# Output stage of a hybrid attention step: loads in another order, x rows filled into y earlier, seven piece places

## The chip, the cores and the metric

The kernel runs on one core of a Trainium2 chip. The metric is the device time of one execution, in microseconds (us). The kernel before took 1928.67 us as the median of three runs (1927.08 to 1930.82). The profile comes from one further execution, which took 1934.61 us; the span of its trace is 1932.9 us.

The engines are called by the names of the profile: PE is TensorE (matmul), DVE is VectorE, ACT is ScalarE, POOL is GpSimd, and SP is SyncE, which here does nothing but wait and issue DMAs. SPq and POOLq are the queues on which SP and POOL issue theirs.

## What is computed

One layer of a trunk, for 1024 new tokens (prompt) and 32 tokens of a running stream (sample), width 2048, all in float32:

```python
hp = rms_norm(y_prompt, norm_pre[l])
mp, st_p = mixers_prompt(hp, w_in[l], attn_sinks[l], rel_bias[l], slopes)
y_prompt = y_prompt + rms_norm(jnp.einsum('btm,md->btd', mp, w_out[l]), norm_post[l])
# the same for y_sample, with the caches of keys and values
```

The mixers project with `w_in` and run three groups of heads: A (stick-breaking attention over the whole past, 12 heads), B (a sliding window with 12 query and 4 key heads) and C (a band of chunks, 8 heads). Each head output is gated by a SiLU. The gated rows are the input of the product with `w_out`. The outputs are `y_prompt`, `y_sample` and twelve tensors of keys and values.

## The kernel before, in words

**Units and ticks.** The attention works two heads at a time: six units of A, then four of C, then six of B. PE runs the projection with `w_in` without a pause, and the attention steps of a unit are placed between its pieces. Python tables give each step a time in ticks, twelve to a projected tile, and the functions `pe_plan`, `act_plan`, `dve_plan` and `sp_plan` sort each engine's instructions by these times. A time only sets the order in the program. When an instruction runs is decided by the semaphores it waits for, and each engine takes its instructions strictly in order.

**The output stage.** After the last tile (`TICKS`) comes the product of the mixed rows (tokens by 2048) with `w_out`. It is cut into two by two blocks and made with seven block products in place of eight (`ORDER`, `LEFT`, `RIGHT`): five of the seven need a sum or difference of two blocks of `w_out`. Each block product is two stages of 512 output columns, each stage is eight *pieces* of 128 inner rows, so there are 14 x 8 = 112 pieces. I call them piece 0 to 111, and "time P(r)" is when PE starts piece r. Stages 0 and 1 are product 3, stages 2 and 3 product 6, then 1, 2, 4, 5 and 7. The last eight pieces (from `TAIL0` = 104) run by another order, with their own buffers (`tail_raw`).

For one piece PE does four groups of three matmuls (`out_mm(r, j)`, j = 0 to 3, one for each 128 tokens): float32 is split into a high and a low part, and hi x hi, hi x lo and lo x hi are added up in PSUM. A stage uses four of seven PSUM banks in turn. So the group j = 3 of a stage's first piece writes the bank which j = 0 of the stage just finished has left, and it must wait until ACT has copied that bank (`copied`, semaphore `c_copied`) or DVE has added it to the result (`added`, `c_added`).

**The path of a piece.** SP loads 256 KB of `w_out` into a place of a ring (`piece_out`: `w_raw` for places 0 to 3, `r_extra` for the rest, `R_RING` = 6 in all), and for products with a sum a second 256 KB into `b_out` (`B_RING` = 5). DVE adds the two (`summed_out`), ACT makes the high part (`high_out`), DVE the low part (`low_out`), and PE waits for it (`operands_out`). SP may load piece r when PE is done with piece r - `R_RING` (`wait_used`).

**What else is loaded.** The mixed rows come back from a scratch tensor in nine loads (`mixed_load`, tile `raw`; places 0 to 7 of it are the first half of the inner dimension, 8 to 15 the second). Products 3 and 6, the pieces 0 to 31, read places 0 to 7 only. The sample tokens are multiplied apart: after 16 of the pieces (`SAMPLE_AFTER`) PE runs `sample_out(v)` with 1 MB of `w_out` rows (`rows_out`, tile `w_s`, one buffer). `post_gains` loads the weights of the last norm. `fill_y` copies x rows 512 to 1023 and the sample rows from DRAM to DRAM into y, because for these rows POOL later adds the normed product onto y with an accumulating DMA (`add_y`). For rows 0 to 511 x is loaded (`residual`) and added by DVE (`finish`).

**What sets the order around the change.** `output_tasks` gives every step of the output stage its time. `piece_out_at(r)` and `mixed_at(n)` are the times of the loads on SP, `at_piece(r)` is the time of piece r. `FINISH` is the order in which token tiles are completed (`TT` is the sample).

## Time and profile before

| what | value |
|---|---|
| median of three runs | 1928.67 us |
| the profiled execution, and its span | 1934.61 us, 1932.9 us |
| PE busy in the span | 1891.8 us (98%) |
| DVE, ACT, POOL busy | 1246.4, 673.4, 56.7 us |
| DMA queues: SP's (q1), POOL's (q0) | 64.5%, 2.2% of 16 engines |
| first matmul of the output stage | at 1578.70 us |
| last busy time of PE | ends at 1924.17 us |

Most of the time PE is busy, at full clock. The views to read are therefore those of the few places where it is not: its idle gaps, the granted clock behind them, and what was late there. "DMA share" in a row by stretches is the mean busy share of the core's 16 DMA engines, and GB/s is what they moved.

### The profile page before, as it was taken

How to read it: one execution, taken by the hardware profiler on the slowest of the kernel's cores; microseconds unless marked ns; L12 is line 12 of the kernel's file. 1: busy time of each engine (PE TensorE's matmuls, PEld its weight loads, DVE VectorE, ACT ScalarE, POOL GpSimd, SP SyncE). 2: the span in 40 equal slices, each digit the busy share in tenths (PEclk: the TensorE clock that was granted, in tenths of full speed). 3: DMA queues.
4: the chain of work that ended last, by engine and by line, in shares of the span. 5: the costliest groups of instructions: out<-in, count | busy, mean ns of one | idle time of the engine just before them, and what ended most of it. 6: DMA issues, size and time to landing. Idle time of an engine off the chain costs nothing.

```text
span 1932.9 us, 31215 instructions
## 1 busy us (share of the span) xinstructions
PE 1891.8 (98%) x12592; PEld 1735.3 (90%) x12592; DVE 1246.4 (64%) x2235; ACT 673.4 (35%) x1235; POOL 56.7 (3%) x119
## 2 busy tenths in 40 slices
PE   6999999999999999999999999999999999999998
PEld 5999999999999999999999999999999987776776
DVE  7368787887878778454454444465445576765878
ACT  7233334343334334122222122233223353334463
POOL 4000000000000000000000000000000000000150
PEclk9999999999999999999999999999999999999999
DMA  6456777776776777666657666465446568766696
GB/s 245 117 121 137 161 159 163 147 152 150 150 163 149 164 149 162 140 140 153 134 126 158 138 141 136 113 147 126 101 100 135 135 246 313 242 228 240 222 256 229
DMA packets 887368, 318.35 MB, mean 165 GB/s; under 512 B 623417, under 2 KB 850505, under 8 KB 883881
## 3 DMA queue, kind: packets, MB, share of 16 engines
q1 hardware_dynamic: 884152, 307.64, 64.5%
q0 software_dynamic: 3072, 8.73, 2.2%
q8 instruction: 99, 1.62, 0.4%
q14 instruction: 45, 0.36, 0.1%
HBM read 227.23 MB, written 96.20 MB: 167 GB/s over the span
## 4 chain that ended last, share of the span: by engine, by line
PE 85%; DVE 9%; DMA 3%; ACT 2%; issue 1%; SPq 0%; POOL 0%; DVEq 0%
PE ps L1277 21%; PE ps L1278 20%; PE ps L1279 20%; PE ps L1471 4%; PE ps L1472 4%; PE ps L1473 4%; PE ps L1369 3%; PE ps L1449 3%; PE ps L1419 2%; PE ps L1341 2%; DVE arena L1956 1%; DMA r_extra<-in_w_out_dram 1%; DMA b_out<-in_w_out_dram 1%; DVE act_lo L1823 1%; DVE arena L1816 1%
## 5 line engine op out<-in xcount | busy, mean ns | idle before, releaser
L1277 PE MATMUL ps<-act_hi,w_hi 128*128 128x352 f32 x2688 | 877.8, 327 | 0.8 <-DVE arena L1856 0.8
L1279 PE MATMUL ps<-act_hi,w_lo 128*128 128x352 f32 x2688 | 863.1, 321 | 0.0
L1278 PE MATMUL ps<-act_lo,w_hi 128*128 128x352 f32 x2688 | 862.8, 321 | 0.0
L1277 PEld LDWEIGHTS ps<-act_hi,w_hi 128*128 128x128 f32 x2688 | 504.4, 188 | 21.0 <-issue 15.7
L1278 PEld LDWEIGHTS ps<-act_lo,w_hi 128*128 128x128 f32 x2688 | 505.4, 188 | 0.0
L1279 PEld LDWEIGHTS ps<-act_hi,w_lo 128*128 128x128 f32 x2688 | 504.4, 188 | 0.0
L1583 ACT ACTIVATE w_hi<-w_raw 128x512 fp32r<-128x512 f32 x224 | 139.4, 624 | 371.7 <-DMA w_raw<-in_w_in_dram 371.5
L1831 DVE TENSOR_TENSOR w_lo<-w_raw,w_hi 128x512 fp32r<-128x512 f32 x224 | 150.4, 672 | 52.8 <-ACT w_hi L1583 52.5
L1650 ACT ACTIVATE arena<-arena,small 128x257 f32<-128x257 f32 (+6 forms) x180 | 101.3, 565 | 198.2 <-DVE small L1994 198.2
L2154 DVE STREAM_TRANSPOSE arena<-arena 128x1024 f32<-128x1024 f32 (+4 forms) x100 | 132.5, 1325 | 38.3 <-ACT arena L1772 37.5
L1772 ACT ACTIVATE arena<-arena 128x1024 f32<-128x1024 f32 (+1 forms) x60 | 61.1, 1019 | 236.4 <-DVE arena L1968 236.4
L1471 PE MATMUL ps<-w_hi,l_hi 128*128 128x512 f32 x280 | 114.0, 407 | 10.4 <-DVE w_lo L2046 3.6
L1472 PE MATMUL ps<-w_lo,l_hi 128*128 128x512 f32 x280 | 111.9, 400 | 0.0
L1473 PE MATMUL ps<-w_hi,l_lo 128*128 128x512 f32 x280 | 111.5, 398 | 0.0
L1994 DVE CUSTOM_DVE_ANT_0 arena<-ps,arena 128x640 f32<-128x640 f32 (+5 forms) x72 | 44.0, 660 | 82.0 <-PE ps L1369 82.0
L1944 DVE TENSOR_TENSOR arena<-ps,arena 128x1024 f32<-128x1024 f32 (+1 forms) x60 | 70.3, 1172 | 29.7 <-ACT arena L1768 29.7
L1859 DVE COPY arena<-ps 128x352 f32<-128x352 f32 x84 | 43.1, 514 | 63.2 <-PE ps L1279 61.6
L1471 PEld LDWEIGHTS ps<-w_hi,l_hi 128*128 128x128 f32 x280 | 54.2, 193 | 31.5 <-issue 15.6
L1956 DVE TENSOR_TENSOR_SCAN arena<-arena 128x512 f32<-128x512 f32 (+4 forms) x102 | 79.5, 833 | 0.8
L1662 ACT ACTIVATE w_hi<-w_raw 128x512 fp32r<-128x512 f32 x70 | 44.0, 629 | 100.7 <-DVE w_raw L2031 84.1
L1764 ACT ACTIVATE arena<-ps 128x1024 f32<-128x1024 f32 (+1 forms) x60 | 58.4, 974 | 51.0 <-DVE ps L1938 40.5
L1768 ACT ACTIVATE arena<-arena 128x1024 f32<-128x1024 f32 (+1 forms) x60 | 61.1, 1019 | 40.7 <-DVE arena L2172 40.3
(173 smaller groups left out, 2073.2 us busy)
## 6 DMA issues: line engine op xcount, KB each, us to landing
w_raw<-in_w_in_dram SPq DMA_DIRECT2D x176, 256.0 KB, 3.4
weight_scratch<-arena SPq DMA_DIRECT2D x216, 128.0 KB, 3.4
arena<-weight_scratch SPq DMA_DIRECT2D x54, 512.0 KB, 4.6
b_out<-in_w_out_dram SPq DMA_DIRECT2D x72, 256.0 KB, 4.3
w_raw<-in_w_out_dram SPq DMA_DIRECT2D x70, 256.0 KB, 3.0
w_s<-in_w_out_dram SPq DMA_DIRECT2D x16, 1024.0 KB, 7.4
w_raw<-in_w_in_dram SPq DMA_DIRECT2D x96, 128.0 KB, 3.1
weight_scratch<-arena SPq DMA_DIRECT2D x80, 132.0 KB, 4.0
```

Source lines behind the costliest of these rows:

```text
L1277: mm(bank(g, GN), wh, ah, start=(k == 0), stop=False)
L1278: mm(bank(g, GN), wh, al, start=False, stop=False)
L1279: last = mm(bank(g, GN), wl, ah, start=False, stop=(k == KT - 1))
L1471: mm(out, th, wh, start=first, stop=False)
L1472: mm(out, th, wl, start=False, stop=False)
L1473: last = mm(out, tl, wh, start=False, stop=end)
L1583: fn(w_hi[:, q, :], w_raw[:, q, :], ACT.Copy).then_inc(hi_made, 1)
L1650: fn(s, s, ACT.Exp, bias=neg_max[0:rows_of(m), t:t + 1], scale=-1.0, accum_out=row_sum[0:rows_of(m), t:t + 1]).then_inc(p_exp, 1)
L1831: v.tensor_tensor(w_lo[:, slot, :], w_raw[:, slot, :], w_hi[:, slot, :].bitcast(F32), ALU.subtract).then_inc(lo_made, 1)
L1944: v.tensor_tensor(both, z, both, ALU.max).then_inc(sp_ready, 1)
L1956: v.tensor_tensor_scan(along, along, along, 0.0 if newest else carry[:, 2 * m - 8 + h:2 * m - 7 + h], ALU.add, ALU.max).then_inc(sum_ready, 1)
L2154: v.transpose(s, s).then_inc(wt_blocks, 1)
```

## The change

The diff does six things.

1. Five of the nine loads of mixed rows (places 8 to 15) move from the times of pieces 1 to 5.9 to those of pieces 8.2 to 17.2, and the load of the norm weights from 9.1 to 30.2.
2. The copies of x rows into y leave SP and the time of pieces 50 to 55. POOL issues them as eight copies of 512 KB and the small sample one while the C units run, each after a certain step of attention (`pv_done`).
3. The ring of pieces has seven places instead of six, so that from piece 10 on each load stands one piece earlier in SP's order, and so do its sum and its low part on DVE and its high part on ACT.
4. The group j = 3 of a stage's first piece is issued after the groups j = 0 to 2 of the second piece.
5. The sample visits come after pieces 15, 19, ..., 75 (every fourth) and not 10, 15, ..., 85 (every fifth); the sample is finished before tiles 4 to 7 and not after them, and takes the inner rows in plain order.
6. The first four loads of x for the last sum (`residual`) move from the times of pieces 99.5 to 102.5 to those of 86.2 to 90.7, 1.5 pieces apart.

```diff
@@ -282,7 +282,7 @@
         return (TICKS - 9, TICKS - 6, TICKS - 3, TICKS, TICKS + 0.2, TICKS + 0.4)[r]
     if r >= TAIL0:
         return at_piece(90.4 + 1.1 * (r - TAIL0))
-    return at_piece(max(r - 5, 2.6 + 0.3 * (r - 6)))
+    return at_piece(max(r + 1 - R_RING, 2.6 + 0.3 * (r - 6)))
 
 
 def summed_at(r):
@@ -290,7 +290,7 @@
 
 
 def mixed_at(n):
-    return (TICKS - 8.9, TICKS - 8.8, TICKS - 5.9, TICKS - 5.8, at_piece(1), at_piece(1.2), at_piece(1.4), at_piece(1.6), at_piece(5.9))[n]
+    return (TICKS - 8.9, TICKS - 8.8, TICKS - 5.9, TICKS - 5.8, at_piece(8.2), at_piece(10.2), at_piece(12.2), at_piece(14.2), at_piece(17.2))[n]
 
 
 def first_left_at(k):
@@ -363,7 +363,7 @@
                 plan.append((at + (1.7 if i else 0.8), "left_lo", i, k))
     for n in range(KT):
         if engine == "sp":
-            plan.append((sample_at(n - 1) if n else at_piece(6), "rows_out", 0, n))
+            plan.append((sample_at(n - 1) if n else at_piece(9.5), "rows_out", 0, n))
     for n in range(NCH):
         if engine == "act":
             plan.append((sample_at(KT - 1) + 0.1 * n, "sample_copy", 0, n))
@@ -396,9 +396,8 @@
                 plan.append((at + 1.2 + 0.1 * half, "add_y", t, half))
     if engine == "sp":
         plan += [(mixed_at(n), "load_mixed", 0, n) for n in range(len(MIXED_LOADS))]
-        plan += [(at_piece(104.3 + 0.1 * n if n > 3 else 99.5 + n), "residual", 0, n) for n in range(len(PLAIN))]
-        plan += [(at_piece(50 + 2.5 * n), "fill_y", 0, n) for n in range(3)]
-        plan += [(at_piece(3.9), "store_mixed", NU - 1, 0), (at_piece(9.1), "post_gains", 0, 0)]
+        plan += [(at_piece(104.3 + 0.1 * n if n > 3 else 86.2 + 1.5 * n), "residual", 0, n) for n in range(len(PLAIN))]
+        plan += [(at_piece(4.2), "store_mixed", NU - 1, 0), (at_piece(30.2), "post_gains", 0, 0)]
     return plan
 
 
@@ -511,9 +510,10 @@
 STAGES = 14
 PIECES = KH * STAGES
 TAIL0 = PIECES - KH
-R_RING, B_RING = 6, 5
+R_RING, B_RING = 7, 5
 LEAD = 3
-FINISH = (4, 5, 6, 7, TT, 0, 1, 2, 3)
+FILLS = 2 * NC
+FINISH = (TT, 4, 5, 6, 7, 0, 1, 2, 3)
 PLAIN = tuple((t, half) for t in range(4) for half in (0, 1))
 ADDED = [(t, half) for t in FINISH for half in (0, 1) if (t, half) not in PLAIN]
 
@@ -526,8 +526,8 @@
 LEFT = {1: ((0, 0), (1, 1)), 2: ((1, 0), (1, 1)), 3: ((0, 0),), 4: ((1, 1),), 5: ((0, 0), (0, 1)), 6: ((1, 0), (0, 0)), 7: ((0, 1), (1, 1))}
 RIGHT = {1: ((0, 0), (1, 1)), 2: ((0, 0),), 3: ((0, 1), (1, 1)), 4: ((1, 0), (0, 0)), 5: ((1, 1),), 6: ((0, 0), (0, 1)), 7: ((1, 0), (1, 1))}
 LEFT_MINUS, RIGHT_MINUS = (6, 7), (3, 4)
-SAMPLE_ORDER = tuple(range(KH, KT)) + tuple(range(KH))
-SAMPLE_AFTER = [10 + 5 * v for v in range(KT)]
+SAMPLE_ORDER = tuple(range(KT))
+SAMPLE_AFTER = [15 + 4 * v for v in range(KT)]
 SAMPLE_BANK = 7
 
 TILE_COPIES = {3: "12", 1: "11", 2: "21"}
@@ -653,9 +653,10 @@
         l_sum = [place(f"l_sum{k}", [P, 512], F32, 0, c + 512) for k, c in enumerate(LEFT_AT)]
         y_s = place("y_s", [P, D], F32, 0, 12736)
         w_s = place("w_s", [P, D], F32, 0, 12736)
-        r_extra = [place(f"r_extra{i}", [P, PIECE], F32, 0, 14784 + PIECE * i) for i in (0, 1)]
-        r_extra_lo = [place(f"r_extra_lo{i}", [P, PIECE], F32R, 0, 14784 + PIECE * i) for i in (0, 1)]
-        r_extra_hi = [place(f"r_extra_hi{i}", [P, PIECE], F32R, 0, 15808 + PIECE * i) for i in (0, 1)]
+        EXTRA_AT = ((14784, 15808), (15296, 16320), (11008, 11520))
+        r_extra = [place(f"r_extra{i}", [P, PIECE], F32, 0, c) for i, (c, _) in enumerate(EXTRA_AT)]
+        r_extra_lo = [place(f"r_extra_lo{i}", [P, PIECE], F32R, 0, c) for i, (c, _) in enumerate(EXTRA_AT)]
+        r_extra_hi = [place(f"r_extra_hi{i}", [P, PIECE], F32R, 0, c) for i, (_, c) in enumerate(EXTRA_AT)]
         ended = [place(f"ended{i}", [P, PIECE], F32, 0, 14784 + PIECE * i) for i in range(4)]
         tail_raw = [place(f"tail_raw{k}", [P, PIECE], F32, 0, ACT_N + 8448 + 1024 * k) for k in range(KH)]
         tail_lo = [place(f"tail_lo{k}", [P, PIECE], F32R, 0, ACT_N + 8448 + 1024 * k) for k in range(KH)]
@@ -1180,14 +1181,6 @@
                 c = slice(1024 * half, 1024 * half + 1024)
                 sp.dma_start(residual_of(n), x_prompt[0, P * t:P * t + P, c].rearrange("p (k c) -> p k c", c=PIECE)).then_inc(res_in[n], 16)
 
-            def fill_y(n):
-
-                if n < 2:
-                    a, b = ((4 * P, 6 * P), (6 * P, 8 * P))[n]
-                    sp.dma_start(y_prompt[0, a:b, :], x_prompt[0, a:b, :]).then_inc(y_filled, 16)
-                else:
-                    sp.dma_start(y_sample[0], x_sample[0]).then_inc(y_filled, 16)
-
             def store_y(t, half):
                 sp.wait_ge(fin_made, PLAIN.index((t, half)) + 1)
                 c = slice(1024 * half, 1024 * half + 1024)
@@ -1242,14 +1235,12 @@
                     post_gains()
                 elif what == "residual":
                     residual(n)
-                elif what == "fill_y":
-                    fill_y(n)
                 elif what == "store_y":
                     store_y(u, n)
 
             sp.wait_ge(k_stored, 128 * (NA + NB + NC))
             sp.wait_ge(v_stored, 32 * (NA + NB + NC))
-            sp.wait_ge(y_filled, 16 * 3)
+            sp.wait_ge(y_filled, 16 * (FILLS + 1))
             sp.wait_ge(y_stored, 16 * len(PLAIN))
 
 
@@ -1541,8 +1532,12 @@
                 out_mm(r, 3)
             for r in range(LEAD, TAIL0):
                 operands_out(r)
-                for j in range(4):
+                for j in range(3):
                     out_mm(r, j)
+                if r % KH == 1:
+                    out_mm(r - 1, 3)
+                if r % KH:
+                    out_mm(r, 3)
                 if r in SAMPLE_AFTER:
                     sample_out(SAMPLE_AFTER.index(r))
             for j in range(4):
@@ -2235,6 +2230,11 @@
             gp.memset(mask_c[64:128, 0:CHUNK], NEG).then_inc(consts, 1)
             pool.wait_ge(consts, CONSTS + 3)
 
+            for n in range(FILLS):
+                pool.wait_ge(pv_done, step_no(NA + n // 2, 1 + 3 * (n % 2)))
+                a, b = (4 * P + n * (4 * P // FILLS), 4 * P + (n + 1) * (4 * P // FILLS))
+                gp.dma_start(y_prompt[0, a:b, :], x_prompt[0, a:b, :]).then_inc(y_filled, 16)
+            gp.dma_start(y_sample[0], x_sample[0]).then_inc(y_filled, 16)
 
             def add_out(r):
                 s, k = divmod(r, KH)
@@ -2273,7 +2273,7 @@
 
             def add_y(t, half):
 
-                pool.wait_ge(y_filled, 16 * 3)
+                pool.wait_ge(y_filled, 16 * (FILLS + 1))
                 pool.wait_ge(scaled, ADDED.index((t, half)) + 1)
                 c = slice(1024 * half, 1024 * half + 1024)
                 y_out = y_prompt[0, P * t:P * t + P, c] if t < TT else y_sample[0, :, c]
```

Two places show what the new times do to the order. The first is SP's queue at the start of the output stage. Before, from the load of piece 4 to that of piece 6 (`r_extra_100` and `r_extra_101` are places 4 and 5 of the ring, `b_out_*` the second operand):

```order
L1140 DMA r_extra_100<-in_w_out_dram 128x512
L1140 DMA b_out_73<-in_w_out_dram 128x512
L1140 DMA r_extra_101<-in_w_out_dram 128x512
L1140 DMA b_out_69<-in_w_out_dram 128x512
L1165 DMA raw<-mixed_scratch 128x2x1056 x2
L1165 DMA raw<-mixed_scratch 128x1056 x2
L1140 DMA w_raw<-in_w_out_dram 128x512
L1140 DMA b_out_70<-in_w_out_dram 128x512
```

The same place after, up to the load of piece 7:

```order
L1141 DMA r_extra_100<-in_w_out_dram 128x512
L1141 DMA b_out_73<-in_w_out_dram 128x512
L1141 DMA r_extra_101<-in_w_out_dram 128x512
L1141 DMA b_out_69<-in_w_out_dram 128x512
L1141 DMA r_extra_102<-in_w_out_dram 128x512
L1141 DMA b_out_70<-in_w_out_dram 128x512
L1141 DMA w_raw<-in_w_out_dram 128x512
L1141 DMA b_out_71<-in_w_out_dram 128x512
```

The four loads of mixed rows (L1165, 3 MB in all) no longer stand between the pieces 5 and 6, and piece 6 has its own place (`r_extra_102`). The four stand behind the pieces 14, 16, 18 and 20 now, and the fifth behind piece 23.

The second is SP's queue some 15 pieces before the end. Before, around the load of piece 96 (the first with a `b_out` there):

```order
L1140 DMA r_extra_101<-in_w_out_dram 128x512
L1140 DMA tail_raw_110<-in_w_out_dram 128x512
L1140 DMA w_raw<-in_w_out_dram 128x512
L1140 DMA b_out_73<-in_w_out_dram 128x512
L1140 DMA tail_raw_111<-in_w_out_dram 128x512
```

After:

```order
L1141 DMA w_raw<-in_w_out_dram 128x512 x2
L1182 DMA raw<-in_x_prompt_dram 128x2x512
L1141 DMA w_raw<-in_w_out_dram 128x512
L1182 DMA raw<-in_x_prompt_dram 128x2x512
L1141 DMA w_raw<-in_w_out_dram 128x512
L1141 DMA r_extra_100<-in_w_out_dram 128x512
L1182 DMA raw<-in_x_prompt_dram 128x2x512
L1141 DMA r_extra_101<-in_w_out_dram 128x512
L1141 DMA b_out_73<-in_w_out_dram 128x512
L1141 DMA tail_raw_113<-in_w_out_dram 128x512
L1182 DMA raw<-in_x_prompt_dram 128x2x512
```

Four loads of 512 KB of x now stand among the loads of the pieces 92 to 97, at the time when POOL adds to y; before they stood behind all pieces.

On PE, the groups at the start of stage 12 (piece 96, `l_hi0`, and piece 97, `l_hi1`). Before, the last two groups of piece 96 and the first of piece 97:

```order
L1471 MATMUL ps<-w_hi_54,l_hi0_74 128x512
L1472 MATMUL ps<-w_lo_53,l_hi0_74 128x512
L1473 MATMUL ps<-w_hi_54,l_lo0_82 128x512
L1471 MATMUL ps<-w_hi_54,l_hi0_74 128x512
L1472 MATMUL ps<-w_lo_53,l_hi0_74 128x512
L1473 MATMUL ps<-w_hi_54,l_lo0_82 128x512
L1471 MATMUL ps<-w_hi_54,l_hi1_75 128x512
L1472 MATMUL ps<-w_lo_53,l_hi1_75 128x512
L1473 MATMUL ps<-w_hi_54,l_lo1_83 128x512
```

After, the third group of piece 97, then the last group of piece 96, then the last of piece 97:

```order
L1462 MATMUL ps<-r_extra_hi2_108,l_hi1_75 128x512
L1463 MATMUL ps<-r_extra_lo2_105,l_hi1_75 128x512
L1464 MATMUL ps<-r_extra_hi2_108,l_lo1_83 128x512
L1462 MATMUL ps<-r_extra_hi1_107,l_hi0_74 128x512
L1463 MATMUL ps<-r_extra_lo1_104,l_hi0_74 128x512
L1464 MATMUL ps<-r_extra_hi1_107,l_lo0_82 128x512
L1462 MATMUL ps<-r_extra_hi2_108,l_hi1_75 128x512
L1463 MATMUL ps<-r_extra_lo2_105,l_hi1_75 128x512
L1464 MATMUL ps<-r_extra_hi2_108,l_lo1_83 128x512
```

So the group that waits for the old bank comes three groups of three matmuls later.

## Rows read from the trace of the kernel before

**Rows 1.** C units, output stage: length, PE, PEld, DVE, ACT, POOL busy, clock, DMA share, GB/s.

```profile
1000.00:1240.00 240.00, 240.00 (x1708) 225.85 (x1708) 111.24 (x245) 54.76 (x121) 0.00 (x0) 1.00 0.62 134
...
1576.00:1933.00 357.00, 336.50 (x1510) 260.88 (x1508) 250.00 (x406) 150.67 (x301) 32.95 (x53) 0.97 0.76 249
```

**Rows 2.** PE in order of time: start, duration, [idle before <- what ended it].

```profile
1599.37 0.77 PE L1471 MATMUL ps<-w_hi,l_hi 128*128 128x512 f32 x1 [3.47 <-DVE w_lo L2046]
1599.94 0.63 PE L1472 MATMUL ps<-w_lo,l_hi 128*128 128x512 f32 x1
1600.36 0.63 PE L1473 MATMUL ps<-w_hi,l_lo 128*128 128x512 f32 x1
...
1756.25 0.76 PE L1471 MATMUL ps<-w_hi,l_hi 128*128 128x512 f32 x1 [3.54 <-ACT raw L1689]
...
1869.28 0.50 PE L1471 MATMUL ps<-r_extra_hi,l_hi 128*128 128x512 f32 x1 [1.23 <-DVE r_extra_lo L2046]
...
1880.37 0.47 PE L1471 MATMUL ps<-w_hi,l_hi 128*128 128x512 f32 x1 [3.27 <-DVE arena L2080]
```

**Rows 3.** Busy time by stretches, as rows 1, around these gaps.

```profile
1589.00:1593.00 4.00, 4.00 (x19) 3.33 (x18) 3.47 (x4) 0.92 (x1) 0.00 (x0) 1.00 1.03 419
...
1599.00:1606.00 7.00, 6.63 (x17) 5.28 (x18) 4.87 (x8) 2.25 (x5) 0.00 (x0) 0.55 0.91 316
...
1756.00:1762.40 6.40, 6.15 (x15) 4.83 (x16) 5.38 (x10) 5.27 (x13) 0.00 (x0) 0.51 0.24 93
...
1868.00:1880.00 12.00, 7.86 (x34) 6.12 (x33) 10.99 (x18) 6.68 (x12) 3.48 (x5) 1.00 1.08 316
1880.00:1884.00 4.00, 3.63 (x12) 2.93 (x13) 4.00 (x8) 1.34 (x3) 1.67 (x2) 0.72 1.08 361
1884.00:1888.00 4.00, 4.00 (x17) 3.25 (x16) 3.43 (x6) 2.08 (x6) 0.86 (x1) 0.85 1.09 302
```

**Rows 4.** DMA issues of SP in order of time.

```profile
1580.27 4.20 SPq L1165 DMA_DIRECT2D raw<-mixed_scratch  x4
1586.42 0.33 SPq L1140 DMA_DIRECT2D w_raw<-in_w_out_dram  x1
...
1622.70 0.33 SPq L1140 DMA_DIRECT2D w_raw<-in_w_out_dram  x1
...
1625.42 0.33 SPq L1140 DMA_DIRECT2D w_raw<-in_w_out_dram  x1
...
1732.30 0.62 SPq L1187 DMA_DIRECT2D out_dram<-in_x_prompt_dram  x1
...
1738.97 0.55 SPq L1187 DMA_DIRECT2D out_dram<-in_x_prompt_dram  x1
```

**Rows 5.** The chain that ended last: start, duration, what.

```profile
1588.25 9.66 DMA b_out<-in_w_out_dram
...
1741.32 12.81 DMA r_extra<-in_w_out_dram
...
1867.08 10.63 DMA b_out<-in_w_out_dram
```

**Rows 6.** `r_extra` loads, issue to landing: 1625 to 1735 us, then 1850 to 1933 us.

```profile
DMA to landing us min/median/max: 2.5/2.9/3.7
...
DMA to landing us min/median/max: 6.8/7.4/7.9
```

**Rows 7.** DMA issues of the page: KB each, median us to landing.

```profile
w_s<-in_w_out_dram SPq DMA_DIRECT2D x16, 1024.0 KB, 7.4
...
out_dram<-arena POOLq DMA_DIRECT2D x4, 512.0 KB, 14.1
```

**Rows 8.** Attention weights of a C unit: landing of the loads (765 to 1200 us).

```profile
DMA to landing us min/median/max: 4.4/5.3/9.0
```

**Rows 9.** One such load on SP, and the matmuls of PE that read it.

```profile
843.09 0.38 SPq L1045 DMA_DIRECT2D arena<-weight_scratch  x1
...
855.89 1.75 PE L1449 MATMUL ps<-arena 128*64 128x128 f32 x28
```

## The prediction, on record before the run

> **What bounds the kernel now.** I read the busy time by stretches first [rows 1]. In the attention stretch PE has no idle time and full clock, so nothing there can be won, only lost. In the output stage, 357 us, PE is idle for 357 - 336.5 = 20.5 us and its clock is 0.97. About 8.8 us of the idle time is the end, where the last tile is finished (PE stops at 1924.17 of 1932.9); the change leaves it alone.
>
> Then PE in order of time [rows 2], for the gaps: 3.47 us before 1599.37, 3.54 before 1756.25, 1.23 before 1869.28, 3.27 before 1880.37. Together 11.5 us.
>
> Then the clock behind each gap [rows 3]. At half clock (1.2 GHz) a matmul starts every 0.42 us (1599.94 to 1600.36) [rows 2]; at full clock (2.4 GHz) a piece of twelve takes 2.72 us, the distance of two loads that each wait for one piece [rows 4], so one takes 0.227. Behind gap 1, 7.0 us at 0.55 lose 3.15 us, less 0.2 for the idle 0.37 in it: 3.0. Behind gap 2, 6.4 us at 0.51 lose 3.1, likewise less 0.1: 3.0. Gap 3 (1.23 us) kept full clock (1868 to 1880 at 1.00). Behind gap 4, 4 x 0.28 + 4 x 0.15 = 1.7. So the stage has lost 3.47 + 3.0 = 6.5, 3.54 + 3.0 = 6.5, and 1.23 + 3.27 + 1.7 = 6.2 us: 19.2 in all. This is the most that the change can win.
>
> Last the chain [rows 5], for what was late. Gap 1: a `b_out` load took 9.66 us. Gap 2: an `r_extra` load took 12.81 us. Gap 4: a `b_out` load took 10.63 us. Undisturbed, such loads land in 2.9 us [rows 6]. All three are crowded DMA engines, and each crowd has its own cause.
>
> **Part 1: mixed rows later, and the seventh place (gap 1).** Four loads of mixed rows, 3 MB, are issued from 1580.27 on; pieces 6 and 7 are issued behind them, piece 6 at 1586.42 when PE has left piece 0, piece 7's `b_out` at 1588.25 (the 9.66 us one) [rows 4, 5]. The engines move 419 GB/s from 1589 to 1593 [rows 3]. In DVE's order the sum of piece 7 stands before the low part of piece 6, so PE waited for piece 7's load already at piece 6: it ran out at 1599.37 - 3.47 = 1595.9, which is P(6). From landing (1597.91) to PE's start it took 1.5 us.
> In the new order the 3 MB are gone from here, 3.2 / 0.4 = 8 us of transfer. Piece 6 has its own place and is issued at about 1580.3. Piece 7 is now the one that waits for piece 0, so its `b_out` goes out at about 1586.8, and the sum of 7 still stands before the low part of 6. The stall is then 1586.8 + L + 1.5 - 1595.9 = L - 7.6 for a load time L. Bounds for L: 2.9 undisturbed [rows 6], no stall; 9.66 as before, 2.1 us, with clock up to 3.5. I take 5, since 2 MB of pieces 3 to 6 are done by then and only 1.5 MB follow: no stall. Gain 6.5 us; at the worst 3.
>
> What hides the moved loads: products 3 and 6 read places 0 to 7 only, so places 8 to 15 are not due before piece 32, and its left sums stand from piece 25 on. The norm weights are first used after stage 6. Both cost nothing.
>
> **Part 2: x rows filled in C's time (gap 2).** The two copies of 2 MB are issued at 1732.30 and 1738.97 [rows 4], and the `r_extra` load behind the second took 12.81 us where its like take 2.9. ACT waits for it in order, so the copy that frees the bank for j = 3 is late. Without the copies nothing heavy is left in that stretch. Gain 6.5 us.
>
> What it costs in C: eight copies of 512 KB, some 50 us apart, where the engines are 0.62 busy [rows 1]. The work closest to its deadline that I find there is the load of the attention weights: issued at 843.09, it lands in 5.3 us (9.0 at worst) [rows 8], and PE reads it at 855.89 [rows 9], so 12.8 - 5.3 = 7.5 us are free. A copy of 2 MB added 12.81 - 2.9 = 9.9 us to a small load; a quarter of it 2.5 us by size. Bounds: 0 below, 9.9 above, which would break 7.5 by 2.4 each time. I take 2.5 and so a cost of zero. On POOL nothing is queued behind these waits until the output stage.
>
> **Part 3: j = 3 later, one piece more of lead (gaps 3 and 4).** Gap 3 is a low part on DVE that came 1.23 us late. A seventh place gives each piece 2.7 us more, and the sample's work, which stood in ACT's and DVE's queues just then, goes to an earlier time: gap 3 goes. Gap 4 is the bank wait of j = 3 at piece 96. In DVE's order the sum for piece 98 stands before the add that frees the bank; now it is the sum for piece 99. Its load is issued at the same moment, P(93), since the ring is one longer and the order one further. From landing to PE's start it took 1880.37 - 1877.71 = 2.66 us. PE wanted the bank at 1880.37 - 3.27 = 1877.10, which is 10.0 us after the issue at 1867.08; now it wants it three groups of three later, 9 x 0.227 = 2.04, so at 12.06. With a load time L the stall is L + 2.66 - 12.06 = L - 9.4. With the old 10.63 that would be 1.2 us.
>
> **Part 4: x for the last sum earlier.** It works against part 3. Two MB are issued between P(86) and P(91) on SP's queue, among the loads of pieces 92 to 97, while POOL's adds to y (512 KB each, 14.1 us [rows 7]) keep the engines full. Against it, the sample's last two loads of 1 MB leave this stretch and the same 2 MB are missing after P(99). Bounds for L: 7.4 us, the loads beside the adds to y alone [rows 6], so no stall; and 14, which is 10.63 plus one 512 KB transfer at the 300 GB/s of the stretch, twice. I take 11.5, near the row that is most like it. Stall 2.1 us, and 0.4 us of clock, between gaps 3 and 4. Gain of parts 3 and 4: 6.2 - 2.5 = 3.7 us; bounds 6.2 and, at L = 14 with 4.6 + 1.7 lost, -0.1.
>
> The Trainium skill's page "DMA: Bandwidth & Descriptors" (section "Queues, rings and completion order") says that on each DMA engine the descriptors of one issuer's ring are consumed in ring order. By that rule a piece behind a load of x waits for all of it, and L would be 10.63 + 1.8 = 12.4, the stall 3.0 us.
>
> **Small costs.** The sample visits now follow every four pieces, 10.9 us, and the 1 MB load takes 7.4 [rows 7]: 3.5 us to spare. Since j = 3 of a stage's first piece is later, `wait_used` for it is 2 us later too; seven places cover that, but a left sum waits for it in DVE's order once in two stages. I put 0.7 us for all this; below zero it can't be, above 3.
>
> **Sum.** -6.5 - 6.5 - 3.7 + 0.7 = -16.0. The profiled execution took 1934.6 us (span 1932.9), so its like would take 1918.6. The median of the runs is 5.9 us under the profiled one. The gaps are in every execution by the order of the queues, so I take the same 16.0 from the median: 1928.7 - 16.0 = 1912.7.
>
> **Rivals.**
> A: the crowd at the end is as bad as before or worse (L about 14). For it speaks that the engines are at 1.08 from 1868 on [rows 3] and the loads of x are added in front. Against it: 2 MB of sample loads go. Gain 6.5 + 6.5 - 0.7 + 0 = 12.3: 1916.4.
> B: the start is crowded again, later. Between P(8) and P(12) SP issues four pieces (2.1 MB), two loads of mixed rows (2.2) and the sample's first (1.05): 5.3 MB in 10.9 us, 490 GB/s, over the 419 of the fullest row. About 1 MB queues up, 2.5 us. Against it: a piece has 6 x 2.72 = 16.3 us from issue to use, less 1.5 for its three steps. A load of 14.8 us would be needed for a stall. If it happens once, with clock, 4 us: 1916.7.
> C, slower than before: the copies in C hit the attention weights. POOL's queue is not behind SP's, so a copy takes its share beside a load which is due. The point from which it decides is 7.5 us of delay. At the upper bound of 9.9, four of the eight copies (those at a unit's second step) stall PE by 2.4 us, and with clock about 5 each; 20 - 16 = 4 us slower: 1933.
> D: the change doesn't do what it says: piece 7 waits for PE as piece 6 did before, and its load is as slow (9.66 us). Then 3.5 us of gap 1 stay, half of what it cost: 1916.2. Against it: the 3 MB that filled the engines are elsewhere.
>
> **Chances.** Forecast 0.57, A 0.22, B 0.08, D 0.05, C 0.04, and 0.04 for no change, if something I don't see eats it. About 0.2% (3.9 us) is what a measurement can tell from no change. Faster by more: 0.57 + 0.22 + 0.08 + 0.05 - 0.03 = 0.89; within: 0.06; slower: 0.05. Range: lower end, all 19.2 won, 1909.5, less 1 for the median's own spread; upper end past A and B together (1920.4) with a little for small costs, 1922.
>
> **What would show it.** Right: no PE gap near pieces 6 and 52, clock 1.00 from 1580 to 1860, `r_extra` loads near 1750 at about 3 us, no PE idle time in the C stretch, and at most one gap under 3 us near piece 96. Wrong: `b_out` loads over 14 us near pieces 14 to 18 or 92 to 98, PE idle in C at the matmuls of line 1449, or DVE (10.99 of 12 us busy from 1868 on [rows 3]) turning into the bound, so that the gaps at the end come back as low parts that are late.

## The result, and the profile after

The changed kernel is 0.2% slower: 1932.45 us (median of 12 runs, 1930.30 to 1933.96) against 1927.70 us of the kernel before on the same chip (12 runs, 1926.22 to 1930.82). The ratio is 1.0022, 95% interval 1.0013 to 1.0030. I had predicted 1912.7 us. The profiled execution took 1933.49 us, its span is 1931.7 us.

I begin as in the prediction, with the busy time by stretches (columns as in [rows 1]).

```profile
1000.00:1240.00 240.00, 240.00 (x1708) 225.82 (x1706) 111.23 (x245) 54.87 (x121) 2.91 (x6) 1.00 0.65 146
1576.00:1932.00 356.00, 334.46 (x1509) 258.54 (x1507) 249.91 (x406) 149.50 (x301) 31.75 (x53) 0.98 0.73 238
```

In the C units PE is as busy as in [rows 1], 240.00 of 240 at full clock, though POOL's copies now run there (POOL has six more instructions, the GB/s rise from 134 to 146). The first matmul of the output stage starts at 1578.59 us, before at 1578.70. In the output stage PE is idle for 21.5 us; in [rows 1] it was 20.5. So the stage keeps its idle time. Where it lies now is seen in PE's rows in order of time (as [rows 2]):

```profile
1642.14 0.50 PE L1462 MATMUL ps<-w_hi,l_hi 128*128 128x512 f32 x1 [0.37 <-DVE l_lo L2046]
...
1646.55 0.50 PE L1462 MATMUL ps<-w_hi,l_hi 128*128 128x512 f32 x1 [1.38 <-DVE l_lo L2046]
...
1841.11 0.79 PE L1462 MATMUL ps<-w_hi,l_hi 128*128 128x512 f32 x1 [2.59 <-DVE l_lo L2046]
...
1871.41 0.54 PE L1462 MATMUL ps<-r_extra_hi,l_hi 128*128 128x512 f32 x1 [4.01 <-DVE l_lo L2046]
...
1875.90 0.47 PE L1462 MATMUL ps<-r_extra_hi,l_hi 128*128 128x512 f32 x1 [0.61 <-DVE r_extra_lo L2041]
...
1881.73 0.61 PE L1462 MATMUL ps<-r_extra_hi,l_hi 128*128 128x512 f32 x1 [3.54 <-DVE arena L2075]
```

I number the gaps of [rows 2] 1 to 4 in order of time. Gaps 1 and 2 (3.47 us near 1599, 3.54 us near 1756) are gone. Six stand in the trace, 12.5 us together. Three of them end in matmuls that start 0.42 us apart and not 0.23: 1.2, 1.4 and 1.6 us of lower clock. Total 16.7 us, against the 19.2 us of the prediction's first part. Four of the six end with `l_lo`, the low part of a *left* operand (mixed rows), which ended none of [rows 2].

**The end.** What SP issues before the gap of 4.01 us, and how long each issue holds the queue (start, duration):

```profile
1850.80 0.46 SPq L1182 DMA_DIRECT2D raw<-in_x_prompt_dram  x1
1851.36 0.42 SPq L1141 DMA_DIRECT2D r_extra<-in_w_out_dram  x1
1851.82 0.46 SPq L1141 DMA_DIRECT2D b_out<-in_w_out_dram  x1
...
1852.82 0.47 SPq L1182 DMA_DIRECT2D raw<-in_x_prompt_dram  x1
...
1857.75 1.95 SPq L1141 DMA_DIRECT2D w_raw<-in_w_out_dram  x1
1859.75 1.48 SPq L1141 DMA_DIRECT2D b_out<-in_w_out_dram  x1
1861.32 4.37 SPq L1141 DMA_DIRECT2D tail_raw<-in_w_out_dram  x1
```

The loads of x (L1182) stand among those of the pieces. The three `b_out` loads issued from 1850 to 1862, from issue to landing:

```profile
DMA to landing us min/median/max: 16.2/16.3/18.3
```

In [rows 5] the one before gap 4 took 10.63 us; I had put 11.5. DVE, in order of time, shows what that does:

```profile
1860.26 0.69 DVE L2041 TENSOR_TENSOR r_extra_lo<-r_extra,r_extra_hi 128x512 fp32r<-128x512 f32 x1
1868.11 0.69 DVE L2026 TENSOR_TENSOR r_extra<-r_extra,b_out 128x512 f32<-128x512 f32 x1 [7.16 <-DMA b_out<-in_w_out_dram]
1868.72 0.68 DVE L2033 TENSOR_TENSOR l_sum<-raw 128x512 f32<-128x512 f32 x1
1870.01 0.69 DVE L2046 TENSOR_TENSOR l_lo<-l_sum,l_hi 128x512 fp32r<-128x512 f32 x1 [0.61 <-ACT l_hi L1662]
```

DVE stands for 7.16 us before the sum of a piece, and behind that sum, in order, are the sum and the low part of a left operand which are due sooner than the piece. PE starts 1.4 us after `l_lo` began.

**Near 1841.** The chain that ended last, up to PE's start:

```profile
1831.78 0.20 POOL small L2272
...
1833.06 1.14 ACT arena L1717
1834.19 0.52 ACT l_hi L1662
1834.71 1.04 ACT raw L1717
...
1837.03 0.62 ACT r_extra_hi L1657
1837.64 0.61 ACT arena L1695 x2
1838.26 0.52 ACT r_extra_hi L1657
1838.78 1.04 ACT raw L1717
1839.81 0.53 ACT l_hi L1662
1840.37 0.70 DVE l_lo L2046
1841.11 0.79 PE ps L1462
```

No DMA is in it. ACT's scaling of finished rows (L1717, 1.1 us each) waits for POOL's short steps, and the high part of a left operand stands behind it. **Near 1642 to 1647** the same view shows a load:

```profile
1629.93 0.38 SPq L1166
...
1630.87 9.90 DMA b_out<-in_w_out_dram
1640.77 0.02 issue
1640.79 0.07 DVE w_raw L2026
1640.86 0.54 issue
1641.40 0.69 DVE l_lo L2046
```

L1166 is the last load of mixed rows; a `b_out` load right behind it takes 9.90 us, and again the low part of a left operand waits in DVE's order behind the sum.

### The profile page after: what moved, and what is told of

Same layout as the page of the kernel before. It is cut to its first block, busy times and chain, and to the rows that moved or that the text cites. A ratio compares the mean times of both kernels' runs of the same rounds, so it can differ in the third digit from the quotient of the medians.

```text
span 1931.7 us, 31221 instructions
## 1 busy us (share of the span) xinstructions
PE 1889.9 (98%) x12592; PEld 1733.2 (90%) x12592; DVE 1246.5 (65%) x2235; ACT 672.7 (35%) x1235; POOL 59.9 (3%) x128
## 4 chain that ended last, share of the span: by engine, by line
PE 86%; DVE 8%; ACT 2%; DMA 2%; issue 1%; POOL 1%; DVEq 0%; SPq 0%; ACTq 0%; POOLq 0%
PE ps L1268 22%; PE ps L1269 20%; PE ps L1270 20%; PE ps L1462 4%; PE ps L1463 4%; PE ps L1464 4%; PE ps L1360 3%; PE ps L1440 3%; PE ps L1410 2%; PE ps L1332 2%; DMA b_out<-in_w_out_dram 1%; DVE arena L1951 1%; DVE act_lo L1818 1%; DVE arena L1811 1%; PE ps L1476 1%
## 5 line engine op out<-in xcount | busy, mean ns | idle before, releaser
L1578 ACT ACTIVATE w_hi<-w_raw 128x512 fp32r<-128x512 f32 x224 | 139.4, 624 | 371.2 <-DMA w_raw<-in_w_in_dram 371.0
L1462 PE MATMUL ps<-w_hi,l_hi 128*128 128x512 f32 x240 | 96.2, 401 | 4.4 <-DVE l_lo L2046 4.3
L1463 PE MATMUL ps<-w_lo,l_hi 128*128 128x512 f32 x240 | 94.2, 393 | 0.0
L1464 PE MATMUL ps<-w_hi,l_lo 128*128 128x512 f32 x240 | 94.1, 392 | 0.0
L1462 PE MATMUL ps<-r_extra_hi,l_hi 128*128 128x512 f32 x176 | 70.5, 401 | 8.2 <-DVE l_lo L2046 4.0
L1657 ACT ACTIVATE w_hi<-w_raw 128x512 fp32r<-128x512 f32 x60 | 37.8, 630 | 96.8 <-DVE w_raw L2026 79.6
```

The lines of the kernel that those rows point to most:

```text
L1462: mm(out, th, wh, start=first, stop=False)
L1463: mm(out, th, wl, start=False, stop=False)
L1464: last = mm(out, tl, wh, start=False, stop=end)
L1578: fn(w_hi[:, q, :], w_raw[:, q, :], ACT.Copy).then_inc(hi_made, 1)
```

## The experiments

Each was timed with the kernel before on the same chip (medians 1929.18, 1928.87 and 1929.70 us for e1 to e4, e5 to e8, e9 to e12); ratios are to it, with 95% intervals. The changed kernel was timed beside a median of 1927.70. So a difference between runs of two such groups, or to the changed kernel, can be off by up to 2 us; where it is small, the gaps in the traces decide and not the times.

**e1: the kernel before, unchanged.** No edit.

> The kernel before, unchanged, for a second profiled execution. Theory 1 (the profiled execution of before was not a typical one: it took 1934.6 us, 7 us over the median of its runs, while that of after took 1 us over its own): the second profile has a span of about 1927 us and lacks about 6 us of the stalls that the first had, most likely one of the gaps at 1599 or 1756 with its slow clock. Rival (profiling itself adds the 7 us, or the gaps are fixed by the order): the span is again 1932 to 1933 us, with gaps of 3.5, 3.5, 1.2 and 3.3 us.

1929.94 us, ratio 1.0005 (0.9996 to 1.0014). The profiled execution took 1928.42 us. Its PE gaps:

```profile
1598.64 0.47 PE L1471 MATMUL ps<-w_hi,l_hi 128*128 128x512 f32 x1 [2.62 <-DVE w_lo L2046]
...
1751.93 0.76 PE L1471 MATMUL ps<-w_hi,l_hi 128*128 128x512 f32 x1 [2.71 <-ACT raw L1689]
...
1868.14 0.47 PE L1471 MATMUL ps<-w_hi,l_hi 128*128 128x512 f32 x1 [0.40 <-issue]
...
1874.17 0.66 PE L1471 MATMUL ps<-w_hi,l_hi 128*128 128x512 f32 x1 [3.71 <-DVE arena L2080]
```

With one of 0.20 that is 9.6 us of idle time, and the clock behind costs 1.0 and 1.6 us: behind the first gap the granted clock is 1.00 (1599 to 1606), where [rows 3] has 0.55. So this execution, the shortest of its eleven, loses 12.2 us and the one I summed from 19.2; both have their large gaps at the same places. Take the loss off the time of each profiled execution and nearly the same floor is left: 1934.6 - 19.2 = 1915.4, 1928.4 - 12.2 = 1916.2, and the changed kernel 1933.5 - 16.7 = 1916.8. Over all executions profiled below, reckoned alike, it lies between 1914 and 1918 us.

**e2: the changed kernel, x loads at the old times.**

```diff
-        plan += [(at_piece(104.3 + 0.1 * n if n > 3 else 86.2 + 1.5 * n), "residual", 0, n) for n in range(len(PLAIN))]
+        plan += [(at_piece(104.3 + 0.1 * n if n > 3 else 99.5 + n), "residual", 0, n) for n in range(len(PLAIN))]
```

> The kernel after, with the four loads of x for the last sum back at the times of pieces 99.5 to 102.5. Theory 1 (these loads, issued among the pieces 92 to 97, made the b_out load of 16.2 us before the gaps of 4.0, 0.6 and 3.5 us at 1871 to 1882, 11.1 us with the clock): it takes 5 to 9 us less than after, 1924 to 1927 us, and the b_out loads there land in 10 to 11 us. Rival (the adds to y and the tail loads fill the engines anyway): 0 to 2 us less than after, gaps of about the same size.

1926.58 us (1926.03 to 1927.26), ratio 0.9986 (0.9977 to 0.9994): 5.9 us below the changed kernel. The `b_out` loads issued from 1850 to 1862 and PE's gaps at the end:

```profile
DMA to landing us min/median/max: 11.4/11.6/12.3
```

```profile
1868.47 0.47 PE L1462 MATMUL ps<-r_extra_hi,l_hi 128*128 128x512 f32 x1 [0.41 <-DVE r_extra_lo L2041]
...
1873.98 0.77 PE L1462 MATMUL ps<-r_extra_hi,l_hi 128*128 128x512 f32 x1 [3.19 <-DVE arena L2075]
```

The early x loads make these loads about 5 us longer, and the gap of 4.01 us is theirs: it is gone here. A gap of 2.60 us near 1840 and one of 0.87 near 1645 stay.

**e3: the changed kernel, the sample's times half undone.** The order of finishing and the visits are put back, but `w_s`'s first load stays at 9.5.

```diff
-FINISH = (TT, 4, 5, 6, 7, 0, 1, 2, 3)
+FINISH = (4, 5, 6, 7, TT, 0, 1, 2, 3)
-SAMPLE_AFTER = [15 + 4 * v for v in range(KT)]
+SAMPLE_AFTER = [10 + 5 * v for v in range(KT)]
```

> The kernel after, with the sample visits after pieces 10, 15, ..., 85 and the tiles finished in the old order; the sample still takes the inner rows in plain order. Theory 1 (the sample's work, put ahead of tiles 4 to 7 on POOL and ACT, delays ACT's high part of the left operand and makes the gap of 2.6 us at 1841, 3.8 us with the clock; and the denser 1 MB loads help to make the gaps at 1642 and 1646): 2 to 5 us less than after. Rival (the sample's end at pieces 85 to 93 comes back into the crowd at the end): the gap at 1841 goes, those near piece 94 grow, and the time is within 1.5 us of after.

1935.19 us (6 runs, 1933.05 to 1936.86), ratio 1.0028 (1.0016 to 1.0039). Much of it is my own edit: with the first visit after piece 10 the load at 9.5 comes too late.

```profile
1614.72 1.08 PE L1476 MATMUL ps<-w_s,raw 128*32 128x512 f32 x4 [5.72 <-DMA w_s<-in_w_out_dram]
```

The gap near 1841 is gone, but this run can't price it. e5, e11 and e12 do.

**e4: the kernel before, with the copies of x rows on POOL in C's time and nothing else.**

```diff
-        plan += [(at_piece(50 + 2.5 * n), "fill_y", 0, n) for n in range(3)]
...
+            for n in range(FILLS):
+                pool.wait_ge(pv_done, step_no(NA + n // 2, 1 + 3 * (n % 2)))
+                a, b = (4 * P + n * (4 * P // FILLS), 4 * P + (n + 1) * (4 * P // FILLS))
+                gp.dma_start(y_prompt[0, a:b, :], x_prompt[0, a:b, :]).then_inc(y_filled, 16)
```

> The kernel before, with only the copies of x rows into y moved: from SP at pieces 50 to 55 to POOL, eight of 512 KB in C's time. Theory 1 (the copies cost 6.5 us in every execution): 5 to 7 us less than before, 1921 to 1923 us. Rival (the gap near piece 52 is there in some executions only, or its time is made up elsewhere): 0 to 2 us less.

1924.60 us, ratio 0.9978 (0.9967 to 0.9989): 4.6 us faster. The gap near 1752 is gone; those near 1598 (2.73 us) and 1870 (3.02 us) stay. The second is gap 4, and this run tells what it is made of. PE's row, and the stretch of 12 us before it:

```profile
1870.35 0.47 PE L1471 MATMUL ps<-w_hi,l_hi 128*128 128x512 f32 x1 [3.02 <-DVE arena L2080]
...
1858.20:1870.30 12.10, 8.44 (x36) 6.30 (x34) 11.28 (x19) 6.74 (x12) 4.32 (x5) 1.00 1.08 316
```

DVE is busy for 11.28 of the 12.1 us, and its rows show no wait for a load in them, only two for ACT (0.19 and 0.62 us); the `b_out` loads issued from 1850 to 1862 take 8.5 to 10.4 us. Gap 4 is there all the same.

**e5: e2, and the sample finished behind tiles 4 to 7.** The visits stay at 15 + 4 v; its squares come 9.5 ticks later, so that the order of times agrees with `FINISH`.

```diff
-        return sample_at(KT - 1) + 2.0 + 0.5 * n
+        return sample_at(KT - 1) + 11.5 + 0.5 * n
-FINISH = (TT, 4, 5, 6, 7, 0, 1, 2, 3)
+FINISH = (4, 5, 6, 7, TT, 0, 1, 2, 3)
```

> The changed kernel with the residual's x loads at the times of before, and the sample's rows finished behind tiles 4 to 7 (their squares 9.5 ticks later; the sample's products stay at 15 + 4 v). Compared with the same kernel that finishes the sample first: 1926.6 us, with a gap of 2.60 us at 1839.8 and 1.2 us of lower clock behind it. Theory (the sample's finish, put ahead of tiles 4 to 7, crowds ScalarE and GpSimd just before the left operands of that region): the gap near 1840 goes, 1922.8 us, up to 1926 if the sample's additions to y now fall among the loads near 1860. Rival (the left operands there are late whatever is finished first, since ScalarE scales tiles 4 to 7 there in both): the gap stays, 1926.6 us.

1921.93 us (1921.12 to 1923.46), ratio 0.9962 (0.9948 to 0.9976): 4.65 us below e2. PE's gaps, all of them:

```profile
1644.32 0.50 PE L1462 MATMUL ps<-w_hi,l_hi 128*128 128x512 f32 x1 [0.35 <-DVE l_lo L2046]
...
1836.83 0.50 PE L1462 MATMUL ps<-w_hi,l_hi 128*128 128x512 f32 x1 [0.97 <-DVE l_lo L2046]
...
1863.86 0.47 PE L1462 MATMUL ps<-r_extra_hi,l_hi 128*128 128x512 f32 x1 [0.21 <-DVE r_extra_lo L2041]
...
1869.38 0.47 PE L1462 MATMUL ps<-r_extra_hi,l_hi 128*128 128x512 f32 x1 [3.20 <-DVE arena L2075]
```

The 2.60 us near 1840 are 0.97, and no lower clock follows them.

**e6: e2, and the last mixed load back at 5.9.**

```diff
-    return (TICKS - 8.9, TICKS - 8.8, TICKS - 5.9, TICKS - 5.8, at_piece(8.2), at_piece(10.2), at_piece(12.2), at_piece(14.2), at_piece(17.2))[n]
+    return (TICKS - 8.9, TICKS - 8.8, TICKS - 5.9, TICKS - 5.8, at_piece(8.2), at_piece(10.2), at_piece(12.2), at_piece(14.2), at_piece(5.9))[n]
```

> The changed kernel with the residual's x loads at the times of before, and the last load of the mixed rows at 5.9 as before, not at 17.2; the four others stay late. Theory (the load at 17.2 stands in front of the weights of left operands and pieces near 1631, which then arrive 9 to 10 us after issue, and the left operands have less slack than a piece): the gap near 1645 goes and 1925.5 to 1926 us are left of 1926.6. Rival (the left operands' own sums wait for ring places or for VectorE there): the gap of 0.9 us stays at 1645. Against the first: the load at 5.9 may bring back part of the gap near 1599.

1925.18 us (1924.68 to 1925.64), 1.4 us below e2. There is no gap near 1645, and none near 1599 came back: the load at 17.2 made that gap. Its worth is less sure than the 1.4 us, since the gap before gap 4 grew from 0.41 us (e2) to 0.94.

**e7: the kernel before, with the order of j = 3 alone.**

```diff
-                for j in range(4):
+                for j in range(3):
                     out_mm(r, j)
+                if r % KH == 1:
+                    out_mm(r - 1, 3)
+                if r % KH:
+                    out_mm(r, 3)
```

> The kernel before with one edit: the fourth product of each region's first piece is issued behind the third of its second piece. Theory of the prediction (TensorE's next region then asks for the first accumulator's successor one piece later): the gap of 1.2 or 0.4 us near 1868 goes and the one near 1880 (3.3 us, or 3.7 near 1874 in the second profile of the kernel before) shrinks by the 1.4 us a piece takes at most: 1927 to 1928.5 us of 1929.2. Rival (the gaps there wait for a piece's operands, not for an accumulator, so the order within a region changes nothing): 1929.2 us, within 0.1%.

1927.02 us, ratio 0.9990 (0.9981 to 0.9999): 1.9 us faster, but not where I had it. The gap near 1752 falls from 2.71 to 0.62 us. The bank wait near 1874 goes too, but in its place stand 2.98 us before 1866.42 (`l_lo`) and five gaps of 0.18 to 0.72 us up to 1888.5: with the clock 6.9 us, against 5.9 in e1.

**e8: the kernel before, with Part 1 alone** (mixed loads and norm weights later, seven places).

```diff
-    return at_piece(max(r - 5, 2.6 + 0.3 * (r - 6)))
+    return at_piece(max(r + 1 - R_RING, 2.6 + 0.3 * (r - 6)))
-    return (TICKS - 8.9, TICKS - 8.8, TICKS - 5.9, TICKS - 5.8, at_piece(1), at_piece(1.2), at_piece(1.4), at_piece(1.6), at_piece(5.9))[n]
+    return (TICKS - 8.9, TICKS - 8.8, TICKS - 5.9, TICKS - 5.8, at_piece(8.2), at_piece(10.2), at_piece(12.2), at_piece(14.2), at_piece(17.2))[n]
-R_RING, B_RING = 6, 5
+R_RING, B_RING = 7, 5
```

> The kernel before with the prediction's Part 1 alone: mixed rows' loads late, norm weights late, seven piece places with pieces issued one earlier; the sample's products, fills, x loads and order of products as before. Prediction's Part 1: minus 6.5 us by the first profile, minus 4 by the second one of before, whose gap near 1599 was 2.6 us at full clock: so 1925.2 us of 1929.2. Theory now (that gap goes, but the mixed loads now delay weights near 1631, 1 to 2 us, and the fill near 1752 still stops TensorE): 1926.5 to 1927.5 us. Rival (the loads at the start only change places): 1929 us or more.

1927.24 us, ratio 0.9993 (0.9984 to 1.0002), 1.6 us and within the error. The gap near 1599 is gone, but the next two are longer than in e1, and there is a new one, of my own making: the first sample visit, after piece 10 as before, reads mixed rows whose load now comes late.

```profile
1609.67 1.06 PE L1486 MATMUL ps<-w_s,raw 128*32 128x512 f32 x8 [0.72 <-DMA raw<-mixed_scratch]
...
1749.82 0.66 PE L1472 MATMUL ps<-w_hi,l_hi 128*128 128x512 f32 x1 [3.38 <-ACT raw L1690]
...
1872.58 0.55 PE L1472 MATMUL ps<-r_extra_hi,l_hi 128*128 128x512 f32 x1 [4.71 <-DVE arena L2081]
```

**e9: e5 and e6 together; e10: that, and the tail loads 2.6 pieces later.**

```diff
-        return at_piece(90.4 + 1.1 * (r - TAIL0))
+        return at_piece(93 + 1.1 * (r - TAIL0))
```

> The two edits of e5 and e6 together: the changed kernel with late x loads, the sample finished behind tiles 4 to 7, the last mixed load at 5.9. If they are independent, e5's 1921.9 minus e6's 1.4 us: 1920.5 us, no gap near 1644, one of about 3.2 us near 1869 and at most 1 us near 1836. Rival (the last gap takes back whatever is gained ahead of it, since the pieces there are late by the clock of the transfers): 1921.9 us and a longer last gap.

> As the one before, and the eight tail loads (and the additions on their arrival) 2.6 pieces later. Theory (the last gap, near 1869, is due to the crowd of tail loads, pieces and y stores, in which b_out takes 11 to 12 us): b_out near 1848 comes back to 9 us or less, the gap shrinks by 2 us or more: 1918 us. Rival 1 (the queues are full whatever stands in them, and only the y stores matter): the gap stays, 1920.5 us. Rival 2 (the tail's pieces are then late themselves): a new gap behind 1880, 1922 us or more.

e9 took 1921.61 us (1921.26 to 1921.80), ratio 0.9961 (0.9948 to 0.9973), as e5 and not 1.4 us below it: the gap near 1644 is gone, but the one near 1864 grew from 0.21 us (e5) to 0.86. e10 took 1921.59 us. Its `b_out` loads issued from 1853 to 1862 take 9.4 to 7.8 us in place of 11.3 to 11.1 in e9, as expected, but the gap does not move:

```profile
1869.24 0.47 PE L1462 MATMUL ps<-r_extra_hi,l_hi 128*128 128x512 f32 x1 [3.19 <-DVE arena L2075]
...
1893.64 0.50 PE L1462 MATMUL ps<-tail_hi,l_hi 128*128 128x512 f32 x1 [1.53 <-DVE tail_lo L2038]
```

Its cause is therefore not the load time of those pieces. In e10 DVE works without a wait for a load from 1857.14 on, with two waits of 0.6 us for ACT, and PE runs out at 1866.05; the instructions that stand before the one which frees the bank are the gap. The second row is the rival that I had named: the tail's operands are now late themselves, by 1.53 us. The clock did not fall behind the 3.19 us this time (1.6 us less than in e9), and so the time is the same.

**e11: the changed kernel with only e5's finish edit; its x loads stay early.**

```diff
-        return sample_at(KT - 1) + 2.0 + 0.5 * n
+        return sample_at(KT - 1) + 11.5 + 0.5 * n
-FINISH = (TT, 4, 5, 6, 7, 0, 1, 2, 3)
+FINISH = (4, 5, 6, 7, TT, 0, 1, 2, 3)
```

> The changed kernel with its early x loads, and only the finish of the sample's rows put behind tiles 4 to 7. With late x loads that edit brought 4.7 us (1926.6 to 1921.9), and late x loads brought 5.9 us. If the two costs add: 1932.45 minus 4.7 = 1927.7 us, with the gaps near 1871 to 1882 as in the changed kernel and at most 1 us near 1840. Rival (the early x loads meet the same y stores either way, and the later y stores make it worse, or the earlier ones were what kept them apart): 1930 us or more.

1927.71 us (1926.81 to 1928.42), the sum expected. With it the two suspects stand in all four combinations:

| | sample finished first | sample finished last |
|---|---|---|
| x loads early | 1932.45 (changed kernel) | 1927.71 (e11) |
| x loads late | 1926.58 (e2) | 1921.93 (e5) |

x costs 5.9 and 5.8 us, the sample's finish 4.7 and 4.65 us; by these medians they add. Taken as differences to the kernel before beside each (+4.75, -1.99, -2.60 and -6.94 us), x costs 7.4 and 5.0 us and the finish 6.7 and 4.3. So that both cost several us is shown, and that they add only to within some 2.4 us.

**e12: e2, and the whole sample part as before** (visits 10 + 5 v, old order of row tiles, `w_s` first at 6, finished last).

```diff
-            plan.append((sample_at(n - 1) if n else at_piece(9.5), "rows_out", 0, n))
+            plan.append((sample_at(n - 1) if n else at_piece(6), "rows_out", 0, n))
...
-SAMPLE_ORDER = tuple(range(KT))
-SAMPLE_AFTER = [15 + 4 * v for v in range(KT)]
+SAMPLE_ORDER = tuple(range(KH, KT)) + tuple(range(KH))
+SAMPLE_AFTER = [10 + 5 * v for v in range(KT)]
```

> The changed kernel with late x loads, and the whole of the sample part as before: products after 10 + 5 v, its row tiles in the old order, w_s's first load at 6, its rows finished behind tiles 4 to 7. What is left of the change is mixed loads and seventh place, fills in C, and the third product later. Theory (new visits cost through the sample's finish alone): 1921.9 us as e5, within 1.5 us. By adding up the parts alone on the kernel before (minus 1.7, minus 4.5, minus 1.9 of 1928.9): 1920.8 us. Rival (the new visit times help by themselves, by fewer loads near the start and the end): 1924 us or more, with a gap near 1600 or a longer one near 1870.

1923.27 us, ratio 0.9968 (0.9956 to 0.9981). It is 1.3 us above e5, and part of that is again a gap of 0.62 us near 1610 where the first visit waits for mixed rows: the new visit times did no harm, the order of finishing did. The three parts together give 6.4 us, alone they gave 1.6 + 4.6 + 1.9 = 8.1; the difference is inside the errors.

## Why the prediction was wrong

**The sum from one execution: failed, 5.9 us.** "The gaps are in every execution by the order of the queues, so I take the same 16.0 from the median." The gaps are, their size isn't (e1: 12.2 us and not 19.2). The profiled execution was 5.9 us above the median because it lost more (19.2 us; over a floor of some 1916, the median leaves room for 13). 16.0 us off that execution gives 1918.6; off the median it gives 1912.7, under the floor of 1914 to 1918 that all profiled executions share (e1). I had both numbers in front of me and took the wrong one.

The rest is read against what I left over. The prediction left 3.2 us of loss (2.5 at the end, 0.7 small costs); the trace after has 16.7. The measured median is 19.8 us above the forecast: 5.9 are this step, 13.5 the loss that I had not left, and the parts below say where it came from.

**Part 1 (gap 1): right about the gap.** It is gone in the changed kernel and in e8. Its worth was 6.5 us in the first profile, 2.6 in e1's. But "Both cost nothing" failed: the last mixed load makes the 0.37 and 1.38 us near 1642 to 1647 (e6). I had worked out the slack of a piece, 16.3 us, and not that of the left operands, which stand behind the pieces' sums in DVE's order. Rival B named this crowd, at 4 us.

**Part 2 (gap 2): right.** The gap is gone, `r_extra` loads there take 2.7 us, and the part alone brings 4.6 us (e4), by e1's profile 3.7. The C units lose nothing, so rival C, which by chance named nearly the measured time, is refuted: PE is busy 240.00 of 240 us. The direction "slower" that it gave came about by something else.

**Part 3 (j = 3 and seven places): failed as to the wait.** "The stall is L - 9.4" makes gap 4 a matter of a load time. I had taken this from the `b_out` load at the start of the chain, 10.63 us in [rows 5], without the row that says how long DVE stood still for it:

```profile
1877.73 0.69 DVE L2031 TENSOR_TENSOR w_raw<-w_raw,b_out 128x512 f32<-128x512 f32 x1 [0.19 <-DMA b_out<-in_w_out_dram]
```

That is 0.19 us, in the kernel before: a quicker load could have taken no more than this off the 3.27 us. In e4 DVE waited for no load at all there, and gap 4 was 3.02 us. In e5, e9, e10 it is 3.2 us, with load times of pieces behind it from 12 down to 8 us. It is the length of DVE's queue once that is late. With the seventh place and the old order of j = 3 it is longer (e8: 4.71 us), the order of j = 3 alone splits it up (e7). The order of j = 3 did help, at gap 2.

**Part 4 (x earlier): the mechanism was right, the size was off.** I took L = 11.5, which is what these loads take without the x loads (11.4 to 12.3 in e2), and a stall of 2.1 us, 2.5 with clock; measured are 16.2 to 18.3, beyond my bound of 14, and 4.01 + 0.61 + 3.54 us with 3.0 of clock, 11.2 in all. Of these the late x loads take away 5.9 (e2). What is left is gap 4, which I had thought gone. Rival A had the crowd, but its price, 4.6 us with 1.7 of clock, was half of what came. By the rule of the Trainium skill's page "DMA: Bandwidth & Descriptors" (section "Queues, rings and completion order") I had worked out L = 12.4; the measured 16.2 lies 3.8 us above what it gave with x counted once.

**Not in the prediction: the sample finished first, 4.7 us.** I had listed its visits under small costs and looked at `w_s` and at `wait_used`, not at ACT and POOL near tiles 4 and 5. The sample's rows are finished at the time of piece 80.5, tiles 4 and 5 at 82.8 and 83.5, and their short steps on POOL and 1.1 us scalings on ACT then meet before the left operands of that product are made (2.59 + 1.2 us near 1841; e5, e11). Of the 2.59 us some 0.95 stay in e5 and e11, so the traces show 2.8 us of gain at this place; the rest of the 4.7 they do not place (with x early the losses at the end are 1.5 us smaller as well, 9.7 in e11 against 11.2), and the 4.7 itself is not sure to better than 2 us.

So the 16.7 us of loss in the trace are 3.8 near 1841, 1.75 near 1645 and 11.2 at the end, where I had left 3.2. By the runs, three parts of the change gain 6 to 8 us and two lose 10.6, which leaves the 4 to 5 us measured. Without these two (e5, e9) the kernel is 7 to 8 us faster than before.

What stays open: what made DVE late before gap 4. In e5, e9 and e10 a `b_out` load of 12 us, issued near 1848, stands ahead of it; in e4 no load does, and the chain ahead runs over POOL's short steps (one of 2.81 us at 1851.80) and ACT's scalings. Whether the gap goes if the adds that free the bank are placed ahead of a sum was not tried.

## What to carry to other kernels

Profile the kernel before more than once, take the loss off the same execution's time and see that it leaves a common floor; a prediction under that floor needs a reason why the floor itself should fall. For each load that is moved, work out the slack of everything that stands behind the waiting instruction on an in-order engine, not of the load's own consumer. When work is moved away from one crowd, list what runs on every engine, the small steps too, at the place it is moved to. And where a chain of waits starts with a load, read how long the engine behind it stood still: a load of 10.63 us can be worth 0.19.

## What the runs showed of the hardware

A gap of one length costs different amounts. Behind 2.62 us near 1599 the granted clock stayed at 1.00 (e1), behind 2.73 us there it fell and cost 1.6 us (e4: 0.66 from 1598 to 1603), and behind 3.47 us it was 0.55 for 7 us [rows 2, 3]; behind 2.71 us it cost 1.0 us, behind 3.20 us 1.6 us (e5), behind 3.19 us in e10 nothing, and 4.71 us (e8) no more than 3.71 (e1), 1.6 us.

SP's own issues can become slow. The stretch before the gap of 4.01 us in the changed kernel:

```profile
1850.00:1860.00 10.00, 10.00 (x46) 8.28 (x45) 8.25 (x14) 2.92 (x6) 0.00 (x0) 1.00 1.07 244
```

In it and just behind, four issues that otherwise take 0.33 to 0.48 us took 1.48 to 4.37 us, and each of them holds back the loads behind it on SP. The DMA share does not tell this: in e4 it is 1.07 from 1851 to 1861 too, and no issue there takes more than 0.46 us. So a full share alone does not make issues slow; e4 has no x loads among the pieces, but it differs in more than that. With x loads of 512 KB among the pieces the median landing of `b_out` was 16.3 us, without them 11.6 (e2).
